# A two-layer diffusion trunk on one core: spatial normalisation on GpSimd, attention one step deeper, block copies earlier in ScalarE's order, gate sums of layer 1 in an earlier stage

## What the kernel computes

```python
for l in range(2):
    ms = split(silu(c) @ ada_w[l] + ada_b[l], 6)         # modulation of the latent tokens
    mc = split(silu(c_ctx) @ ada_w[l] + ada_b[l], 6)     # and of the context tokens
    p = modulate(rmsnorm(x), ms[0], ms[1]) @ w_in[l]     # 2560 columns: q, k, v, u, gv
    q, k = rope(q), rope(k)                              # latent tokens
    s1, s2 = softmax(q1 k1' / 8), softmax(q2 k2' / 8)    # 4 heads, two score maps each
    a = rmsnorm((s1 - lam * s2) @ v, subln_g) * (1 - lambda_init)
    s = u * (w_s @ layernorm(gv, sg_ln_g, sg_ln_b) + b_s)    # spatial gating, in chunks of 128 tokens
    x = x + ms[2] * rmsnorm(concat(a, s) @ w_out[l], post_mix_g)
    y = swiglu(f) if l == 0 else top2_of_8_experts(f)        # f: x normed, modulated by ms[3], ms[4]
    x = x + ms[5] * rmsnorm(y, post_ffn_g)
```

## Time and profile before

| | |
|---|---|
| runs | 1889.41 us median of 3 (1885.5 to 1889.56) |
| profiled execution | 1885.67 us, span 1883.7 us |
| TensorE (PE), matmuls | 1729.6 us busy, 92% |
| TensorE, weight loads (PEld) | 1398.9 us, 74% |
| VectorE (DVE) | 1420.7 us, 75% |
| ScalarE (ACT) | 1098.8 us, 58% |
| GpSimd (POOL) | 41.4 us, 2% |
| granted TensorE clock, mean | 0.967 of full speed |
| moved by DMA | 505.79 MB, 269 GB/s in the mean |

### The profile page before, as it was taken

One profiled execution on the slowest core, in us unless ns is written; L12 is line 12 of the kernel. 1 busy time (PEld: TensorE's weight loads), 2 busy tenths in 40 slices (PEclk: granted clock), 3 DMA queues, 4 the chain that ended last, 5 costly groups with the idle time before them and its releaser, 6 DMA issues.

```text
span 1883.7 us, 24259 instructions
## 1 busy us (share of the span) xinstructions
PE 1729.6 (92%) x8008; PEld 1398.9 (74%) x8008; DVE 1420.7 (75%) x1669; ACT 1098.8 (58%) x1409; POOL 41.4 (2%) x73
## 2 busy tenths in 40 slices
PE   6998798999999969875999999999999999999993
PEld 3765576878878757554788888888888888888883
DVE  3846757565664484763799999999999999999994
ACT  3344434222222253443788888888888888888883
POOL 0110000000010000101000000000000000000000
PEclk9999999999999989986999999999999999999997
DMA  9945134565674434443799999999999999999992
GB/s 316 255 123 189 56 125 155 191 215 179 201 247 147 129 105 147 123 149 132 278 391 354 396 380 371 392 353 395 380 368 390 360 387 386 361 394 358 391 376 93
DMA packets 229520, 505.79 MB, mean 269 GB/s; under 512 B 16376, under 2 KB 47248, under 8 KB 229184
## 3 DMA queue, kind: packets, MB, share of 16 engines
q1 hardware_dynamic: 225216, 493.30, 73.3%
q0 software_dynamic: 4224, 11.47, 2.3%
HBM read 497.34 MB, written 19.96 MB: 275 GB/s over the span
## 4 chain that ended last, share of the span: by engine, by line
issue 54%; PE 34%; DVE 7%; ACT 3%; DMA 2%; SPq 0%; POOL 0%; POOLq 0%; ACTq 0%; DVEq 0%
PE ps L571 10%; PE ps L573 10%; PE ps L572 10%; DVE w_lo L1340 1%; DMA raw<-in_ffn_w 1%; PE ps L800 1%; DVE att L1598 1%; ACT w_hi L1041 1%; PE ps L640 1%; DVE xs L1519 1%; DMA raw<-in_ada_w 1%; DVE acc L1356 1%; DVE hT_lo L1492 1%; DVE pr L1593 0%; ACT pr L1165 0%
## 5 line engine op out<-in xcount | busy, mean ns | idle before, releaser
L1340 DVE TENSOR_TENSOR w_lo<-raw,w_hi 128x1024 fp32r<-128x1024 f32 x570 | 685.1, 1222 | 213.4 <-ACT w_hi L1041 179.5
L1252 ACT ACTIVATE w_hi<-raw 128x1024 fp32r<-128x1024 f32 x448 | 473.9, 1062 | 105.8 <-PE ps L573 105.8
L571 PE MATMUL ps<-w_hi,he_hi 128*128 128x512 f32 x896 | 354.4, 395 | 0.7 <-DVE he_lo L1747 0.7
L573 PE MATMUL ps<-w_hi,he_lo 128*128 128x512 f32 x896 | 350.0, 391 | 0.0
L572 PE MATMUL ps<-w_lo,he_hi 128*128 128x512 f32 x896 | 349.3, 390 | 0.0
L1340 DVE TENSOR_TENSOR w_lo<-raw_more,w_hi 128x1024 fp32r<-128x1024 f32 x224 | 274.0, 1225 | 45.7 <-ACT w_hi L1252 26.0
L1252 ACT ACTIVATE w_hi<-raw_more 128x1024 fp32r<-128x1024 f32 x224 | 237.8, 1063 | 53.5 <-PE ps L573 53.5
L1041 ACT ACTIVATE w_hi<-raw 128x1024 fp32r<-128x1024 f32 x122 | 128.6, 1062 | 213.4 <-PE ps L573 196.5
L573 PEld LDWEIGHTS ps<-w_hi,he_lo 128*128 128x128 f32 x896 | 168.5, 188 | 36.0
L571 PEld LDWEIGHTS ps<-w_hi,he_hi 128*128 128x128 f32 x896 | 168.7, 188 | 34.8 <-issue 1.0
L572 PEld LDWEIGHTS ps<-w_lo,he_hi 128*128 128x128 f32 x896 | 168.8, 188 | 33.9
(11 more groups left out here) (222 smaller groups left out, 1980.0 us busy)
## 6 DMA issues: line engine op xcount, KB each, us to landing
raw<-in_moe_w SPq DMA_DIRECT2D x448, 512.0 KB, 6.0
raw_more<-in_moe_w SPq DMA_DIRECT2D x224, 512.0 KB, 6.1
raw<-in_ada_w SPq DMA_DIRECT2D x96, 512.0 KB, 4.5
raw<-in_ffn_w SPq DMA_DIRECT2D x66, 512.0 KB, 5.0
raw<-in_w_in SPq DMA_DIRECT2D x40, 512.0 KB, 5.2
raw<-in_w_out SPq DMA_DIRECT2D x16, 512.0 KB, 5.6
yrows<-in_x SPq DMA_DIRECT2D x8, 512.0 KB, 7.8
xe<-xrows SPq DMA_DIRECT2D x8, 512.0 KB, 6.6
```

Of the source, the lines that this page charges most:

```text
L571: pe.matmul(o, lh, rh, start=start, stop=False)
L573: return pe.matmul(o, ll, rh, start=False, stop=stop)
L1252: act.activation(w_hi[:, s % SPL, :], expert_raw(i), ACT.Copy).then_inc(hi_done, 1)
L1340: dve.tensor_tensor(w_lo[:, s_ % SPL, :], src, w_hi[:, s_ % SPL, :].bitcast(F32), ALU.subtract)\
```

## The change

Five things are changed together.

1. **Normalisation.** The three 128x512 instructions per block move from VectorE to GpSimd (`spatial_norms`, one after the other for all blocks of a layer, linked by semaphores). VectorE keeps one reciprocal for all blocks, at step 10 (layer 0) or 6 (layer 1), whose semaphore `ln rstd` starts them. On ScalarE the root that this reciprocal needs now stands before the wait of the head norm's root, not behind it.
2. **Deeper attention.** `LAG` = 2: step t transposes the weights of item t-2 and multiplies those of item t-3; the loop has three tail steps instead of two. There are three score buffers; the third lies where row 0 of `acc` lies.
3. **Early copies.** ScalarE copies a projection block behind the exps of the odd step t in which TensorE ends it, not at the head of step t+1.
4. **Layer 1's gate sums.** In the q, k, v stage of layer 1 two acc units follow a projection unit instead of one (`acc(1 + l)`): `GATES[2]` goes first, then `GATES[3]`, which is gathered in row 1 of `acc`. The units leave the attention. The sum of `GATES[3]` moves to step 3 of the attention on TensorE (bank `BANK_MIX`), its two VectorE instructions to step 5.
5. **One gate row.** All gates use the row `arow` (before, the gates of layer 1 had a row of their own); the first mix of a layer waits until it is read, and SP waits for all gate rows to be written out before the first expert load.

```diff
+LAST_GATE_STEP = 3
+LAG = 2
-NORM_AT = {0: (10, 11, 12, 13), 1: (6, 7)}
+NORM_AT = {0: 10, 1: 6}
...
+def acc_row(i, r):
+
+    return 1 if i == GATES[3] else min(r, streams(i) - 1)
...
                 project(j, u, u + 1)
-                acc(1 if 3 <= 4 * jn + u < 11 else 0)
+                acc(1 + l if 3 <= 4 * jn + u < 11 else 0)
...
-            acc(1 if l and t >= 2 else 0)
             step_end[l, t] = len(units)
...
-        pr = place("pr", [P, 2, 2, 512], F32, Z + 40960)
+        pr_two = place("pr", [P, 2, 2, 512], F32, Z + 40960)
+        pr_one = place("pr_one", [P, 2, 512], F32, A)
+        pr = [pr_two[:, 0], pr_two[:, 1], pr_one[:, :, :]]
...
             sp.wait_ge(sg("cat"), HEADS * (NB + NLAT))
+            sp.wait_ge(sg("gate out"), 64 * len(GATES))
             experts(0)
...
+            def link(ins):
+
+                links[0] += 1
+                ins.then_inc(sg("pool ch"), 1)
+                pool.wait_ge(sg("pool ch"), links[0])
+
+            def spatial_norms(l):
+
+                pool.wait_ge(sg("params in"), 16 * (11 + 3 * l))
+                pool.wait_ge(sg("ln rstd"), l + 1)
+                for b in out_blocks(l):
+                    v = proj[:, b, 4 * DA:5 * DA]
+                    link(pool.tensor_scalar(v, v, st[:, 48 + 2 * b:49 + 2 * b], st[:, 36 + b:37 + b], ALU.subtract, ALU.mult))
+                    link(pool.tensor_tensor(v, v, lng_bc[:, :], ALU.mult))
+                    pool.tensor_tensor(v, v, lnb_bc[:, :], ALU.add).then_inc(sg("vn"), 1)
...
             gate_params(1)
+            spatial_norms(0)
             pool.wait_ge(sg("vn"), NB)
...
                     pe.wait_ge(sg("ada fin"), len(ADA_SEQ))
+                    pe.wait_ge(sg("gate row"), 1 + 3 * l)
                     pe.wait_ge(sg("wsT"), l + 1)
...
+                    if l and t == LAST_GATE_STEP:
+                        pe.wait_ge(sg("wsT"), 2)
+                        acc_sum(GATES[3], BANK_MIX)
                     if ada_slot(l, t - 1):
                         ada_turn(ada_slot(l, t - 1), BANK_ADA)
-                    if 1 <= t <= n:
-                        i = t - 1
+                    if LAG <= t < n + LAG:
+                        i = t - LAG
...
-                    if t >= 2:
-                        i = t - 2
+                    if t > LAG:
+                        i = t - LAG - 1
...
                     if j == 3:
                         pe.wait_ge(sg("ada fin"), len(ADA_SEQ))
-                        pe.wait_ge(sg("gate row"), 1 if l == 0 else 3)
...
-                if l:
-                    acc_sum(GATES[3], ADA)
                 us = at["out", l, 1]
...
-                    if t >= 2 and t % 2 == 0 and t <= 4 * nb:
-                        c = t // 2 - 1
-                        j, b = ug[l][c]
+
+                    if t < n:
+                        nk = 512 if its[t][0] < NLAT else 256
+                        act.wait_ge(sg("rowmax"), 16 * l + t + 1)
+                        if t >= 3:
+                            act.wait_ge(sg("wT ps"), 16 * l + t - 2)
...
+                    if t % 2 and t < n:
+                        j, b = ug[l][t // 2]
...
                         act.activation(proj[:, b, 512 * j:512 * j + 512], ps[:, BANK_UG, :], ACT.Copy).then_inc(sg("proj%d" % l), 1)
...
+                            if i // HEADS == nb // 2 - 1:
+                                act.wait_ge(sg("ln ms"), l + 1)
+                                act.activation(st[:, 44:44 + nb], st[:, 40:40 + nb], ACT.Sqrt).then_inc(sg("ln rt"), 1)
                             act.wait_ge(sg("o ms"), NB * l + i // HEADS + 1)
...
-                    if n == 0:
-                        dve.wait_ge(sg("wsT ps"), 1)
-                    row = gate_row[n]
-                    link(dve.tensor_tensor(row[:, :], ps[:, bank, :], ab_bc[:, :], ALU.add))
-                    dve.tensor_tensor(row[:, :], row[:, :], pg_bc[:, :], ALU.mult).then_inc(sg("gate row"), 1)
+                    if n % 2 == 0:
+                        dve.wait_ge(sg("wsT ps"), n // 2 + 1)
+                    link(dve.tensor_tensor(arow[:, :], ps[:, bank, :], ab_bc[:, :], ALU.add))
+                    dve.tensor_tensor(arow[:, :], arow[:, :], pg_bc[:, :], ALU.mult).then_inc(sg("gate row"), 1)
...
+                    if l and t == LAST_GATE_STEP + 2:
+                        part_row(GATES[3], BANK_MIX)
...
-                    if t in NORM_AT[l]:
-                        i = NORM_AT[l].index(t)
-                        if i == 0:
-                            dve.wait_ge(sg("ln rt"), l + 1)
-                            dve.wait_ge(sg("params in"), 16 * (11 + 3 * l))
-                        spatial_norm(l, i)
-
...
+                    if t == NORM_AT[l]:
+                        dve.wait_ge(sg("ln rt"), l + 1)
+                        dve.wait_ge(sg("params in"), 16 * (11 + 3 * l))
+                        dve.reciprocal(st[:, 36:36 + nb], st[:, 44:44 + nb]).then_inc(sg("ln rstd"), 1)
...
                 split_upto(last_s(("out", l, 1)))
-                if l:
-                    part_row(GATES[3], ADA)
```

More of the change, by code:

```diff
@@ L236, in program @@
         lnb_bc = place("lnb_bc", [P, SG], F32)
+        A = end[0]
         acc = place("acc", [P, 2, UW], F32)
@@ L242, in program @@
         st2 = place("st2", [P, 128], F32)
-        att = place("att", [P, 2, 8], F32)
+        att = place("att", [P, 3, 8], F32)
         flag = place("flag", [P, 1], I32)
@@ L521, in gate_rows @@
                 for q in range(4):
-                    pool.dma_start(grows[n, q:q + 1, :], gate_row[n][32 * q:32 * q + 1, :]).then_inc(sg("gate out"), 16)
+                    pool.dma_start(grows[n, q:q + 1, :], arow[32 * q:32 * q + 1, :]).then_inc(sg("gate out"), 16)
                 pool.wait_ge(sg("gate out"), 64 * (n + 1))
@@ L549, in _ @@
             gate_params(3)
+            spatial_norms(1)
             gate_rows(3)
@@ L623, in acc_sum @@
                         m = pe.matmul(ps[32 * q:32 * q + 32, bank, :], ones[:, 0:32],
-                                      acc[:, min(r, streams(i) - 1), 512 * half:512 * half + 512], start=True, stop=True,
+                                      acc[:, acc_row(i, r), 512 * half:512 * half + 512], start=True, stop=True,
                                       tile_position=(0, 32 * q))
@@ L756, in attend @@
                 n = len(its)
-                for t in range(n + 2):
+                for t in range(n + LAG + 1):
                     if t < n:
@@ L1150, in _ @@
                         act.activation(wsT[:, :], ps[:, BANK_MIX, :], ACT.Copy).then_inc(sg("wsT"), 1)
-                    if t >= 2 and t % 2 == 0 and t <= 4 * nb:
-                        c = t // 2 - 1
-                        j, b = ug[l][c]
+                    if t < n:
[3 more added lines that the diff above has]
+                            act.wait_ge(sg("wT ps"), 16 * l + t - 2)
+                        for m_ in range(2):
+                            act.activation(pr[t % 3][:, m_, 0:nk], scores(l, t)[:, m_, :], ACT.Exp, scale=SCALE,
+                                           bias=att[:, t % 3, 2 + m_:3 + m_], accum_out=att[:, t % 3, 4 + m_:5 + m_])\
+                                .then_inc(sg("exp"), 1)
+                    if t % 2 and t < n:
+                        j, b = ug[l][t // 2]
                         if b == out_blocks(l)[-1]:
@@ L1156, in _ @@
                         else:
-                            act.wait_ge(sg("ug part"), 2 * (NB - 1) * l + (nb - 1) * (c // nb) + b + 1)
+                            act.wait_ge(sg("ug part"), 2 * (NB - 1) * l + (nb - 1) * (t // 2 // nb) + b + 1)
                         act.activation(proj[:, b, 512 * j:512 * j + 512], ps[:, BANK_UG, :], ACT.Copy).then_inc(sg("proj%d" % l), 1)
-                    if t < n:
-                        nk = 512 if its[t][0] < NLAT else 256
-                        act.wait_ge(sg("rowmax"), 16 * l + t + 1)
-                        if t >= 2:
-                            act.wait_ge(sg("wT ps"), 16 * l + t - 1)
-                        for m_ in range(2):
-                            act.activation(pr[:, t % 2, m_, 0:nk], scores(l, t)[:, m_, :], ACT.Exp, scale=SCALE,
-                                           bias=att[:, t % 2, 2 + m_:3 + m_], accum_out=att[:, t % 2, 4 + m_:5 + m_])\
-                                .then_inc(sg("exp"), 1)
                     if t in (2 * nb - 1, 2 * nb):
                         split_upto(at["in", l, IN_ORDER[4]][2 * (t - (2 * nb - 1)) + 1].s)
-                    if 1 <= t <= n:
-                        i = t - 1
+                    if LAG <= t < n + LAG:
+                        i = t - LAG
                         nk = 512 if its[i][0] < NLAT else 256
@@ L1349, in gather_part @@
                 if k == 0 and i:
-                    dve.wait_ge(sg("acc sum"), i)
+                    dve.wait_ge(sg("acc sum"), i - (i == GATES[3]))
                 for r in range(n):
+                    total = acc[:, acc_row(i, r), :]
```

(19 more changed lines are left out.)

28 lines of the change are left out of this document (9 added, 19 removed).

## The result

The changed kernel takes 1876.53 us (median of 5, 1875.87 to 1879.34), the kernel before 1886.35 in the same number of runs: a ratio of 0.9945, 95% interval [0.9934, 0.9955]. So 10 us are gained, faster by more than 0.2%, where 15.8 were forecast; 1876.5 lies in the range of 1864 to 1883 and, 4.5 us above the 1872 that was named, still in the forecast's own case (1865 to 1879).

What follows compares the result with a forecast made beforehand. TensorE sets the pace, with 22.3 and 22.2 us of waits in the attention stages plus half clock. Savings of 3.6 (layer 0), 11.2 (layer 1) and 1.0 (output projection) make 15.8: 1869.9 to 1873.6, named 1872 us, range 1864 to 1883.

Steps and rivals of the forecast that it cites:

- the forecast's own case: The whole kernel takes between 1865 and 1879 us; chance 0.60.
- Its own signs: Block-copy waits at most 2.5 us, no transposes waiting for weights, GpSimd rows near 1.2, VectorE unstretched, q, k, v stage 62.
- the four things that it said would make it wrong: GpSimd rows passing 2 us, first mix waiting over 4, clock falling as often as before, q, k, v stage growing.
- The gate sums: Layer 1's accumulations move to the q, k, v stage, priced at nothing there; 10 us leave attention, output projection loses 1.0.
- The waits: TensorE's remaining waits in attention: 14.9 us instead of 22.2 in layer 1, 19.5 instead of 22.3 in layer 0.
- the bank: Layer 1's attention: transposes wait 2.6 us for the copy of their bank, which stands behind the last exps.
- The half clock: TensorE in attention: half clock costs 2.5 us instead of 8.6 in layer 1, and 1 in layer 0.
- the hold of 1.2: Attention: GpSimd holding up VectorE costs 2.4 us, 1.2 in each layer.
- GpSimd's instructions: Normalisation in attention: 18 instructions of 128x512 at 1.2 us each, making the first mix wait 1.0 us per layer.
- the rival: GpSimd holds VectorE over a shared port: 3 us more in layer 0, 4 in layer 1, total 1880 us; chance 0.17.
- The depth: Attention: transposes two steps behind the scores remove weight waits of 3.3 and 7.7 us, for one more tail step.
- the late transposes: Attention tail: transposes wait behind the copy of their bank, 3.0 us in layer 0 and 2.6 in layer 1.

Runs made afterwards that it cites:

- the first four below it in the table: Changed kernel with normalisation left out (0.9933), written to an unread row (0.9963), back on VectorE (0.9953), or last transposed-weight copy ahead of the exps (0.9932).
- no_norm: Changed kernel with the spatial normalisation left out, its reciprocal kept; 0.9933 of the kernel before, layer 0 118.4 us, layer 1 69.2.
- order_defer: Changed kernel with the last transposed-weight copy ahead of the last exps, one gating a step earlier, and VectorE's root-dependent work behind the row maximum; 0.9909 of the kernel before.
- the late roots: Changed kernel one step deep, with head scaling and the norm's reciprocal moved behind the next step's weights and row maximum; 0.9898 of the kernel before.
- lag_one: Changed kernel with the attention one step deep again, third score buffer kept; 0.9895 of the kernel before, layer 0 119.5 us, layer 1 65.5.

## Why the prediction came out as it did

**Faster: right; where: right but for layer 0.** Layer 1's attention gains 9.2 (forecast 11.2), layer 0's none (forecast 3.6), the q, k, v stage none (forecast none), the output projection 1.8 (27.1 to 25.2; forecast 1.0).

**Its own signs: mixed.** The q, k, v stage kept its length, no block copy is waited for longer than 2.3 us, no transposes wait for weights, and the first mix waits under 4. But of the four things that it said would make it wrong, GpSimd's rows do pass 2 us (the scaling), and in layer 0 the clock falls as often as before (0.97 both times); and VectorE's scaling and weights did not keep 0.49 and 0.75. That the time still lies in the forecast's own case owes something to that case being 14 us wide.

**The gate sums: right.** 46 us of VectorE and 238 GB/s were forecast for the q, k, v stage, 45.1 and 239 came, at the same length. Undone, they cost 6.0 us in the attention and 1.5 in the output projection.

**The waits: right in sum in layer 1, short in layer 0.** Of the 14.9 us laid out for layer 1, 15.0 came (17.4 less the 2.4 ahead of the scores), 0.6 and 2.3 at the u blocks, 2.9 at the bank for 2.6, 1.5, 0.5, 4.3 for 4.1. The first mix took 2.7 instead of 1.0, the copy 0.2 instead of 1.7 and the first block none instead of 0.5: that these cancel is luck. In layer 0 it is 22.6 for 19.5: 2.2 instead of 1.0 at the mix, 4.0 instead of 3.2 at the end, 6.1 instead of 5.0 at copies.

**The half clock: the mis-sized term.** The sum gave back 6.1 of the 8.6 us that half clock cost in layer 1, because the long waits ahead of the slow stretches would go. They went, and others of 2.7 to 4.3 us took their place in the tail, with a clock of 0.61 behind the first two. TensorE is busy for 54.0 us on 48.5 of work: 5.5 lost, 3.0 more than allowed. That is, within 0.2, the 2.0 by which layer 1 is longer than forecast and the hold of 1.2, which the forecast had added besides and which cost nothing there. In layer 0 the 98.9 busy us are as many as before, where 97 were forecast. 1.9 of this and 3.1 of waits, less the hold of 1.2, are the 3.8 by which that stage is longer than forecast.

**GpSimd's instructions: 1.66 in the mean for 1.2.** The products lie near it, the scaling at 2.32 doesn't; a first block takes 4.8 us instead of 3.6, and that is the mix's wait. The Trainium skill, GPSIMD Engine Reference, section Performance versus the Vector engine, gives 1.96 for tensor_tensor; here 1.27 and 1.39 against 0.69 are 1.8 and 2.0, so the trace agrees for the products.

**The hold: the rival's place, less than half of its price.** VectorE's weights stretch while GpSimd multiplies, and the norm's whole price is 3.1 us in layer 0 (the rival: 3 more than the forecast there) and none in layer 1 (the rival: 4). The rule of the Trainium skill, SBUF — State Buffer, section Who interferes with whom, holds for GpSimd's products; the rows above show it. For GpSimd's scaling the rows at the end of this document differ from it, and they decide.

**The depth: right as a sum, wrong as a part.** The waits for weights went, as forecast, and the 3.0 and 2.6 of the late transposes were in the sum. What the prediction didn't do is lay the rows out without the depth: it called the price "one more step at the tail" and took 7.7 and 3.3 us as the gain. One step deep, with all else changed, is 2.0 and 3.6 us shorter and 0.5% in the run; alone, the depth is worth nothing.

**Still open.** Why the clock stays at 1.00 in one tail and falls in another of like waits was not taken apart; what was measured is that in layer 1 five variants (the changed kernel and the first four below it in the table) with waits of 13.7 to 15.8 us end within 0.3 us of each other (69.1 to 69.4), the ones with less waiting having more busy time. For no_norm the rows above show the place; for the others it was not followed.

## What to carry to other kernels

A wait taken out of the middle of a pipelined stage is won only if the tail behind the last item doesn't get longer by it: cut the stage at its last item and compare both pieces. A change of several parts should be summed once without each part; the part that looked best here was the one that cost. An engine that stands on another's table load with ready work behind it is found in its timeline as one long idle ahead of a tiny instruction. With the depth, reordering it together with two other orders took 0.4% off the changed kernel (order_defer), and the offload gave nothing that the runs can tell; one step deep it was the other way round (the offload 0.3%, the late roots alone nothing). What an order is worth hangs on the others.

## What was not expected of the hardware

A scaling by two column scalars took 2.07 to 2.51 us on GpSimd, 0.55 on VectorE, while a product or a sum of two 128x512 tiles took 1.27 and 1.39 in the mean, and 0.69 on VectorE. And the scaling didn't always hold VectorE as the products do: without the depth (lag_one), VectorE's weights ran at 0.49 and 0.75 beside one of 2.07 (GpSimd's timeline, then VectorE's). The sum here ends 0.3 us after the scaling; the next pair, at 806.07 and 806.59, has the same lengths and lies beside the next scaling (805.26 to 807.33) from start to end.

```profile
800.38 2.07 POOL L529 TENSOR_SCALAR proj<-proj,st 128x512 f32<-128x512 f32 x1 [30.22 <-DVE st L1652]
802.54 1.39 POOL L530 TENSOR_TENSOR proj<-proj,lng_bc 128x512 f32<-128x512 f32 x1
```

```profile
801.50 0.49 DVE L1618 TENSOR_SCALAR pr<-pr,att 128x512 f32<-128x512 f32 x1
802.02 0.75 DVE L1619 SCALAR_TENSOR_TENSOR pr<-pr,att 128x512 f32<-128x512 f32 x1
802.69 1.22 DVE L1624 TENSOR_REDUCE att<-ps 128x2 f32<-128x1024 f32 x1
```

The last line is the row maximum, which reads PSUM: its 1.22 are unstretched though a GpSimd product runs from 802.54. A scaling can hold VectorE all the same: in the changed kernel a sum of 1.15 us lies inside a scaling of 2.25 (from 199.08). And it may go both ways: in the changed kernel all three scalings of 2.51 us began while a stretched sum of VectorE had 0.56 us to go. Why one sum is held by a scaling and another is not stays open.
